# A transformer pair in fp32 on one core: the residual stream and four projections laid out by token

## The reference

```
# first block
h = rmsnorm(x, pre_mix_g) * (1 + scale_a) + shift_a        # mod = silu(c) @ w_mod + b_mod
proj = h @ w_in                                            # 5952 columns
mix = concat([latent_attention(proj), gated_recurrence(proj)]) @ w_out
x = x + gate_a * rmsnorm(mix, post_mix_g)
h = rmsnorm(x, pre_mlp_g) * (1 + scale_m) + shift_m
y = square(relu(h @ w_up)) @ w_down                        # 8192 wide
x = x + gate_m * rmsnorm(y, post_mlp_g)
# second block
u = rms_norm(x, mix_pre_g_2)
merged = sigmoid(ga) * (attention(u) @ w_attn_o) + sigmoid(gb) * conv(u)
x = x + rms_norm(merged @ w_out_2, mix_post_g_2)
u = rms_norm(x, ffn_pre_g_2)
f = (silu(gate) * up) @ w_down_2                           # 5632 wide
x = x + rms_norm(f, ffn_post_g_2)
```

## Time and profile before

| | us |
|---|---|
| median of three runs | 2996.82 |
| lowest and highest of them | 2993.32, 3002.66 |
| the profiled execution | 2995.96 |
| its span, first to last instruction | 2994.2 |
| PE busy in it | 2751.9 (92%) |
| DVE busy | 1968.1 (66%) |
| ACT busy | 1201.4 (40%) |

### The profile page before, as it was taken

One profiled execution on the slowest core, in us unless ns is written; L12 is line 12 of the kernel. 1 busy time (PEld: TensorE's weight loads), 2 busy tenths in 40 slices (PEclk: granted clock), 3 DMA queues, 4 the chain that ended last, 5 costly groups with the idle time before them and its releaser, 6 DMA issues.

```text
span 2994.2 us, 41611 instructions
## 1 busy us (share of the span) xinstructions
PE 2751.9 (92%) x14939; PEld 2350.7 (79%) x14939; DVE 1968.1 (66%) x2489; ACT 1201.4 (40%) x1521; POOL 22.6 (1%) x42
## 2 busy tenths in 40 slices
PE   2299898699799999999979999999979999999998
PEld 2288797567688888888868878887768888888886
DVE  6899685569888445664464878867565565565444
ACT  2134323334444334444344434454444444444433
POOL 1000000000000000000010000000000000000000
PEclk7599899789899999999989999999989999999999
DMA  9799432329487556665546555555536666656554
GB/s 320 254 366 367 150 113 55 108 77 324 155 282 261 177 189 185 188 184 186 179 131 185 176 171 153 164 163 164 171 96 191 184 183 188 188 182 204 182 184 147
DMA packets 491558, 563.46 MB, mean 188 GB/s; under 512 B 17943, under 2 KB 434131, under 8 KB 491072
## 3 DMA queue, kind: packets, MB, share of 16 engines
q1 hardware_dynamic: 489824, 558.18, 58.4%
q0 software_dynamic: 1632, 3.89, 0.6%
HBM read 559.90 MB, written 2.10 MB: 188 GB/s over the span
## 4 chain that ended last, share of the span: by engine, by line
PE 78%; DVE 10%; DMA 8%; ACT 2%; issue 2%; DVEq 0%; SPq 0%; ACTq 0%
PE ps L653 42%; PE ps L655 21%; DMA w_raw<-in_w_in 5%; PE ps L688 3%; PE ps L689 3%; PE ps L690 3%; DMA w_raw<-in_w_mod 2%; PE ps L843 2%; DVE w_lo L1265 2%; DVE mod_acc L1307 2%; ACT w_hi L996 1%; DVE mod_acc_a L1541 1%; PE ps L793 1%; PE ps L720 1%; DVE rstd L1385 1%
## 5 line engine op out<-in xcount | busy, mean ns | idle before, releaser
L653 PE MATMUL ps<-acts,w_hi 128*128 128x512 f32 x4976 | 1780.8, 402 | 46.0 <-DVE acts L1403 15.5
L1265 DVE TENSOR_TENSOR w_lo<-w_raw,w_hi 128x1024 fp32r<-128x1024 f32 (+1 forms) x872 | 1055.1, 1213 | 737.6 <-ACT w_hi L996 601.3
L655 PE MATMUL ps<-acts,w_lo 128*128 128x256 f32 x4976 | 1400.7, 281 | 0.0
L996 ACT CAST w_hi<-w_raw 128x1024 fp32r<-128x1024 f32 (+1 forms) x784 | 814.5, 1042 | 1198.5 <-PE ps L655 1044.5
L653 PEld LDWEIGHTS ps<-acts,w_hi 128*128 128x128 f32 x4976 | 941.3, 189 | 288.3 <-issue 45.6
L655 PEld LDWEIGHTS ps<-acts,w_lo 128*128 128x128 f32 x4976 | 946.5, 190 | 2.1 <-issue 1.7
L653 PE MATMUL ps<-ff,w_hi 128*128 128x512 f32 x1024 | 361.7, 397 | 0.0
L655 PE MATMUL ps<-ff,w_lo 128*128 128x256 f32 x1024 | 288.4, 282 | 0.0
L653 PEld LDWEIGHTS ps<-ff,w_hi 128*128 128x128 f32 x1024 | 193.4, 189 | 45.5
L1307 DVE SCALAR_TENSOR_TENSOR mod_acc<-mod_w,silu_c,mod_acc 128x512 f32<-128x512 f32 (+1 forms) x300 | 192.8, 643 | 9.4 <-DVE mod_acc L1307 0.6
L655 PEld LDWEIGHTS ps<-ff,w_lo 128*128 128x128 f32 x1024 | 193.9, 189 | 0.1
(11 more groups left out here) (244 smaller groups left out, 1612.8 us busy)
## 6 DMA issues: line engine op xcount, KB each, us to landing
w_raw<-in_w_in SPq DMA_DIRECT2D x236, 512.0 KB, 4.4
w_raw<-in_w_down SPq DMA_DIRECT2D x216, 512.0 KB, 3.5
w_raw<-in_w_gate_up SPq DMA_DIRECT2D x176, 512.0 KB, 3.6
mod_w<-in_w_mod SPq DMA_DIRECT2D x128, 512.0 KB, 8.3
w_raw<-in_w_up SPq DMA_DIRECT2D x128, 512.0 KB, 4.1
w_raw<-in_w_mod SPq DMA_DIRECT2D x64, 512.0 KB, 5.2
w_raw<-in_w_out SPq DMA_DIRECT2D x64, 512.0 KB, 4.8
w_raw<-in_w_attn_o SPq DMA_DIRECT2D x16, 512.0 KB, 3.4
```

The costliest lines, as they stand in the source:

```text
L653: pe.matmul(ps[:, bank, :], hi, lin_.act[:, kk, :, :], start=at_first, stop=False, skip_group_check=True)
L655: mm = pe.matmul(ps[:, bank, 0:T], lo, lin_.act[:, kk, 0, :], start=False, stop=at_last, skip_group_check=True)
L996: act.copy(w_hi[:, slot, 0:kn, 0:lin_.width], w_raw[:, slot, 0:kn, 0:lin_.width]).then_inc(hi_ready, 1)
L1265: dve.tensor_tensor(low[cut], raw[cut], high[cut].bitcast(F32), ALU.subtract).then_inc(lo_ready, 1)
```

## The change

The residual is kept as `x_tok`, with tokens on partitions. w_o, down_0, down_1 and out_2 become token panels of 512 columns as down_2 was: kind "tokens" weighs the result by a row of gains on its way out of PSUM and squares it on ScalarE with a sum along the free axis; "tokens_part" (down_0) copies it, "tokens_add" (down_1) adds it, squares it and weighs it one panel later. The row of gains, the same in each partition, is made by `spread_row`: 16 matmuls of a column, broadcast, against the identity; ScalarE keeps it (`keep_row`). A statistic is now two columns (128 tokens by two halves). `boundary` makes the root, adds eight pieces of 128x512 to the residual while ScalarE squares them, makes the second root, scales the stream to `xh` (ScalarE, `turn_norm`) and `turn` transposes it on TensorE, two transposes for a tile of features; `turn_high` and `turn_low` make hi and lo out of PSUM. Tiles 0 to 7 are turned ahead of the next phase, 8 to 11 and 12 to 15 behind its first two chunks. At the start x is normed between the two sections of the modulation and turned there (`x_turned`). The pieces of `w_mod` beside w_o are 2 rows of 512 columns instead of 4 of 256. A load of ScalarE's table for the square root (`load_root`) is put ahead of the places that need it.

```diff
-            Phase("w_o", panels // 2, [(w_o, 0, 2), (w_o, 1, 2)], Side(4, 4, 8)),
+            Phase("w_o", 1, [(w_o, i, 0) for i in range(4)], Side(2, 4, 4)),
...
-            Phase("down_0", panels // 2, [(down[0], 0, 2), (down[0], 1, 2)]),
+            Phase("down_0", 1, [(down[0], i, 0) for i in range(4)]),
...
-                if ph.name in out_norm and not first:
-                    n = out_norm[ph.name]
-                    for i in range(2):
-                        done = (it * 2 + (b - 2)) * 2 + i
-                        pe.wait_ge(*n.squared(done + 1))
-                        pe.matmul(ps[:, 5, 0:T], ones[:, :], ring[:, 2 * b + i, :], stop=False,
-                                  start=opens and b == i == 0,
-                                  skip_group_check=True).then_inc(n.added.sem, 1)
...
+            def turn(t, tiles):
+
+                for k in tiles:
+                    if k >= 4:
+                        pe.wait_ge(*(t.ring if t.shift else t.lo)(k - 3))
+                    pe.wait_ge(*t.scaled(2 * (k // 4) + 2))
+                    for half in range(2):
+                        mm = pe.transpose(ps[:, 4 + k % 4, half * P:(half + 1) * P],
+                                          t.xh[:, half, k * P:(k + 1) * P], ident)
+                    mm.then_inc(t.turned.sem, 1)
+
+            def spread_row(o):
+
+                for k in range(DT):
+                    mm = pe.matmul(ps[:, 4 + k // 4, (k % 4) * P:(k % 4 + 1) * P],
+                                   o.gain[:, k:k + 1].to_broadcast([P, P]), ident, start=True, stop=True)
+                mm.then_inc(o.row_mm.sem, 1)
...
+                if ph.name in turns and first and j < 2:
+                    turn(turns[ph.name], range(4 * j + 8, 4 * j + 12))
...
             def before_up_0():
                 pe.wait_ge(summed, summed_all("w_o"))
-                norm(n_y1, DT - 4)
                 pe.wait_ge(side_products, side_all("w_o"))
                 sum_mods(mod_acc, 2)
-                norm(n_x2)
+                pe.wait_ge(mods_done, 10)
+                turn(t_2, range(8))
 
             def before_down_0():
                 pe.wait_ge(side_products, side_all("up_0"))
                 sum_mods(mod_acc, 2)
+                pe.wait_ge(gate_ready, 2)
+                spread_row(o_2)
...
+            def turn_norm(t, o=None):
+
+                for i, half, cut in pieces():
+                    if o:
+                        act.wait_ge(*o.added(i + 1))
+                    if i:
+                        act.wait_ge(*t.squared(i))
+                    act.activation(square, x_tok[:, half, cut], ACT.Square,
+                                   accum_out=x_sums[:, half, i // 2:i // 2 + 1]).then_inc(t.squared.sem, 1)
+                root(x_root[:, :], t.stat)
+                act.wait_ge(*t.stat(3))
+                for i, half, cut in pieces() if o else sorted(pieces(), key=lambda p: p[1]):
+                    act.activation(t.xh[:, half, cut], x_tok[:, half, cut], ACT.Identity,
+                                   scale=x_root[:, half:half + 1]).then_inc(t.scaled.sem, 1)
...
+            def token_evict(ph, b):
...
+                if kind == "tokens_part":
+                    dve.tensor_copy(o.y[:, :, cut], ps[:, bank:bank + 2, :]).then_inc(summed, 1)
+                elif kind == "tokens_add":
+                    dve.tensor_tensor(o.y[:, :, cut], o.y[:, :, cut], ps[:, bank:bank + 2, :],
+                                      ALU.add).then_inc(summed, 1)
+                    if b:
+                        weigh(o, b - 1)
...
+            def residual(o, to):
+
+                for i in range(8):
+                    quarter, half = divmod(i, 2)
+                    cut = slice(quarter * NW, (quarter + 1) * NW)
+                    dve.scalar_tensor_tensor(to[:, half, cut], o.y[:, half, cut], y_root[:, half:half + 1],
+                                             x_tok[:, half, cut], ALU.mult, ALU.add).then_inc(o.added.sem, 1)
...
             def before_up_0():
-                dve.wait_ge(summed, summed_all("w_o"))
-                gate_gain("post_mix_g", 2)
-                norm(n_y1)
-                residual(r_y1, gains)
                 take_mods(2, 8)
                 scale_gain("pre_mlp_g", 4)
-                norm(n_x2)
-                apply(a_x2)
+                boundary(o_1, t_2, "w_o")
+                turn_low(t_2)
```

More of the change, by code:

```diff
@@ L951, in before_gate_up, with before_out_2 @@
             def before_gate_up():
-                pe.wait_ge(summed, summed_all("out_2"))
-                norm(n_y2, DT - 4)
-                norm(n_x4)
+                turn(t_4, range(8))
+            def before_out_2():
+                pe.wait_ge(extra, extra_all("conv_o"))
+                spread_row(o_3)
             hooks = {
@@ L1040, in root, with squares @@
                 act.activation(ap, ap, ACT.Sqrt).then_inc(stat.sem, 1)
-            def squares(n, residual=None, first=0):
-                for k in range(first, n.tiles):
-                    if residual and k % 4 == 0:
-                        act.wait_ge(*residual.added(k // 4 + 1))
+            def squares(n):
+                for k in range(n.tiles):
                     if k >= 4:
@@ L1383, in invert_root, with boundary @@
+            def boundary(o, t, phase):
+                inverse_root(y_sums, y_root[:, :], o.stat, o.squared)
+                dve.wait_ge(summed, summed_all(phase))
+                residual(o, x_tok)
+                inverse_root(x_sums, x_root[:, :], t.stat, t.squared)
             def invert_root(ap, stat):
```

467 lines of the change are left out of this document (247 added, 220 removed).

## The result

The changed kernel takes 2952.51 us, median of four runs (2947.86 to 2960.04), the kernel before beside it 2995.07 (2989.85 to 3002.66): a ratio of 0.9863, 95% interval 0.9834 to 0.9892. The forecast was 2970 with a range down to 2957. The profiled execution took 2949.73 us, its span is 2947.9.

The account below looks back on a forecast made before the run. The prediction took the kernel as a stream of TensorE matmuls, with DMA or VectorE setting the pace in places and 97 us in three boundaries. Its terms summed to -26.5 us, giving 2970 us; 8-in-10 range 2957 to 2984.

Parts of the forecast that it names:

- The matmul stream: down_0, down_1, out_2: matmuls by token at 2.80 us a chunk instead of pairs; +3.4 and -0.8, together +2.6 us.
- norm matmuls: Ones-matmuls summing squares inside down_1 and out_2 go away, 0.76 us a group: -7.6 us.
- w_o: Stage from attention's last head to the last main matmul: TensorE becomes the beat, 99.1 to 94.2 us, -4.9.
- Boundary 1: w_o to up_0, last main matmul to first of the next projection: 30.1 against 36.7 us, -6.6.
- Rival C: up_0's weights come late if w_o's stream stays at 366 GB/s or under; boundary 1 gives nothing: 2976 us, chance 0.12.
- The term for transposes: Boundary 1: transposes of tiles 8 to 15 among the first panel's chunks hold the stream 1.4 us, with waits 1.8.
- Boundaries 2 and 3: down_1 to in_c, 23.9 against 30.2 us, -6.3; out_2 to gate_up, 21.6 against 30.1 us, -8.5; transposes included.
- down_0 and out_2: take_mods, gate and spread_row delay down_0, +4.7 us; spread_row outlasts the idle time in out_2, +1.5 (bounds 0 and 5.5).
- Rival B: spread_row in down_0 and out_2 and three boundaries' transposes run at half clock behind pauses: +12 us, 2982, chance 0.14.
- down_2 and tail: down_2: spread_row 3.8 us replaces eight groups of transposes at 0.36, +0.9; tail: table load moved ahead, -0.9 us.
- Input: Cheaper high and low parts of t_1, -2.1 us, less 0.7 for w_mod loads delayed by x's statistic: -1.4.

Follow-up runs that it names:

- before_160: The kernel before with 160 unused bytes ahead of the shared buffers, giving them the changed kernel's addresses: 2979.41 us, ratio 0.9928 to the kernel before.
- after_unaligned: The changed kernel with 32 unused bytes ahead of the shared buffers, 32 bytes off a multiple of 64: 2966.55 us, ratio 0.9923 to the kernel before.
- rows_inside: The changed kernel with the rows of w_o, down_0, out_2 and down_0's modulation sums moved into the matmul stream: 2961.83 us, ratio 0.9875 to the kernel before.
- turns_between: The changed kernel with transposes of tiles 8 to 15 one behind each of the first eight tiles' matmuls: 2953.74 us, one execution.
- before_again: The kernel before, unchanged, profiled a second time: 2997.87 us, one execution.
- big_384: The changed kernel with 128 unused bytes ahead of the shared buffers: 2944.01 us, one execution.

## Why the prediction was wrong

The path by which the change gains was right; what failed is a step that the prediction did not have. It took each stage whose code is not changed at its old time, and so at zero, without a reason; these stages and the input gave some 17 of the 46 us between the two profiles. That the sum for the touched stages came near (-25.1 for -28.9) is partly luck: the misses on single terms, which follow, are up to 11 us and cancel.

- **What it left out.** The change moves the shared buffers by 160 bytes. At like addresses or loads the gain is 20 to 23 us by the times; the rest, about 20, came with the move (before_160, and after_unaligned from the other side). Of this the profiles show the loads of in_h at 387 instead of 367 GB/s, worth some 2 us of in_h in the kernel before. The pitch of pairs in gate_up and up_1 (-11 us in the two profiles) is only in part explained. It varies between executions of one kernel. In gate_up it was the longer in all three profiles of the kernel before with the buffers off a multiple of 256, and the shorter in both on one. But the changed kernel had the shorter at 32 and 128 too, and rows_inside and turns_between the longer at 0. That stays open.
- **The matmul stream, +2.6.** Mis-sized. A chunk by token is 2.72 us in w_o and out_2 (0.2267 a matmul) and 2.79 to 2.80 in down; down_2, the only row of it before, was read at a place that the addresses made slow. And the row for pairs before, 2.77, came from down_0, while down_1 ran at 2.82. With the norm matmuls (-7.6) the two terms came to -16.5 over the three stages instead of -5.0. The largest part that neither term had is the half clock behind a pause: in the kernel before, the first pairs of down_0 and out_2 stood at it, 2.2 and 2.1 us over their pitch, and in the changed kernel the row's matmuls take that stretch.
- **w_o, -4.9.** Right: -4.9.
- **Boundary 1, -6.6.** Wrong; with up_0 it gave 0.6, and at the same pitch of up_0 (before_again, 216.2 us) it lost 2.9. Rival C's result came true, its reason did not: the fourth chunk lands late and the modulation sums begin 9.2 us behind the last matmul's start, not 4.0. But it is late because SP's queue waits for w_o's last modulation product; the boundary is 33.5 to 33.9 us whether in_h loads at 367 or at 387 GB/s. The earlier trace rows had the sign of it, a split that began 7.2 us behind the last matmul. Behind the eviction the sums stood on the path as forecast, and the first matmul of up_0 came at 33.9 instead of 28.3. The term for transposes, 1.8 in up_0's first panel, was 5.6 (185.1 against 179.6 us at the same pitch): VectorE ran dry behind tile 7 while TensorE did the first chunk at half clock (granted 0.50 from 774.8 to 780.5). That was no term of the sum.
- **Boundaries 2 and 3, -6.3 and -8.5.** Right: 23.3 for 22.1 and 20.7 for 19.8 us, -7.0 and -9.4.
- **down_0 and out_2, +4.7 and +1.5.** Rival B for the row: spread_row took 6.79 and 6.20 us, not 3.8; +7.5 and +3.8, inside the bound of 5.5 that was named for out_2. In w_o it took 5.47, at down_2 3.74. But what the prediction held against B was right as well: without the 2.2 and 2.1 us that the first matmuls lost before, the net is +5.3 and +1.7, near the forecast.
- **down_2 and tail, +0.9 and -0.9.** -0.9 and -0.8. The row costs 3.6 us in down_2 and the eight groups of transposes had cost 3.5, not 2.9; the rest is the pitch, 0.2323 us for 0.2334.
- **Input, -1.4.** Not seen as such. in_h's first matmul stood between 129.6 and 133.7 us in five profiles of the kernel before and its padded forms, between 129.8 and 136.2 in eleven of the changed kernel and its forms; the means are 131.8 and 132.0. The start differs by more between executions than the term is large. Behind it something of the kind shows: in_h from its first to its last matmul, at 367 GB/s, is 187.7 to 187.9 us before and 186.2 and 186.5 in after_unaligned and big_384.

## What to carry to other kernels

Before a stage is taken as untouched, compare the addresses of its buffers: a few small tiles ahead of them can move the time by nearly as much as the edit. Put what is loaded at a multiple of 256 bytes, and stationary and moving operands of a matmul at the same distance from one, as these runs bear out. When weights come late, look at what stands ahead of them in the queue before blaming the rate: a stretch at 0 GB/s tells. Small work moved out of a pause did not take the half clock with it here; what came first paid. Judge an edit of a few us by its stage in the trace, not by the whole time, when other stages have two speeds. Work on the path that nobody needs yet (the modulation sums) is moved by one line in the order of the engine that takes it.

## What was unexpected in the hardware

- The loads of in_h run at 386 to 389 GB/s with mod_w at a multiple of 256 bytes, at 367 elsewhere. The Trainium skill (DMA: Bandwidth & Descriptors, section "Where 436 GB/s comes from") puts the limit of HBM for a core at about 358 GB/s; the measurement decides.
- fp32r matmuls of 512 columns at 0.2267, 0.2323 or 0.2334 us from start to start, by the distance of their operands' addresses.
- Pairs of 512 and 256 columns at 0.3467 or 0.3533 us at a granted clock of 1.00, the one or the other for a whole stage, and not the same in two executions of one kernel: up to 9 us in gate_up alone.
